# One decoder step on one core: a weight split shared by two engines, another order of the last projections and their builds, and cache pages queued ahead of a store

## What is computed

```python
h = rms_norm(x, ln_g) @ w_in          # 1024 -> 4168 columns, split into 11 parts
# A) sparse attention: an indexer scores every key, each query keeps 256
score = einsum(relu(iq . ik), iw);  idx = top_k(where(causal, score, -inf), 256)
logits = rms_norm(q) . rms_norm(k)[idx] / 8 + rel_bias[bucket(q_pos - idx)]
a_out = softmax(logits) @ v[idx]      # 8 query heads, 4 key heads of 64
# B) HGRN2 recurrence, 8 heads with a 64x64 state, chunks of positions
f = lb + (1 - lb) * sigmoid(h_f);  S = f * S + (1 - f) (x) h_i;  o = silu(h_q) . S
mix = concat(a_out * silu(a_gate), rms_norm(o) * silu(h_gate))
y = x + mix @ w_out                   # 1024 x 1024
# outputs: y, k, v, ik of prompt and sample, the final state, and the samples' states
```

## Time and profile before

| what | value |
|---|---|
| median of 3 runs | 805.73 us (801.14 to 806.96) |
| the profiled execution | 804.48 us, span 802.8 us |
| mean granted clock of PE | 0.989 of full speed |
| busy share | PE 95%, DVE 68%, ACT 52%, POOL 49% |
| PE idle by the busy time | 802.8 - 760.7 = 42.1 us |
| projections with the recurrence | to about 519 us |
| attention, samples and first output tiles | 519 to about 730 us |
| last output tiles | to the end |

### The profile page before, as it was taken

How to read it: one execution, slowest core, us unless ns; L and a number is a source line. 1 busy time by engine, 2 the same in 40 slices (tenths; PEclk the granted TensorE clock), 3 DMA queues, 4 the chain that set the end, 5 groups by cost and what they waited for, 6 DMA issues and landing times.

```text
span 802.8 us, 20221 instructions
## 1 busy us (share of the span) xinstructions
PE 760.7 (95%) x7576; PEld 704.1 (88%) x7576; DVE 542.8 (68%) x1110; ACT 420.7 (52%) x1274; POOL 396.2 (49%) x576
## 2 busy tenths in 40 slices
PE   3999999999999999999989999979799998999998
PEld 3889989899999999999988999868588878898998
DVE  3644767998999999879994846678446367555121
ACT  6765775346365686577554746554435554422110
POOL 3454735437735693579396435249932427510220
PEclk9999999999999999999999999999999999999999
DMA  8303021221102312231202345594644634341632
GB/s 282 93 21 86 14 90 41 66 66 42 53 3 80 94 47 74 80 95 47 74 28 75 124 127 166 161 253 134 155 153 140 206 122 142 124 139 55 229 101 82
DMA packets 69927, 83.57 MB, mean 104 GB/s; under 512 B 20458, under 2 KB 55962, under 8 KB 69578
## 3 DMA queue, kind: packets, MB, share of 16 engines
q1 hardware_dynamic: 65146, 68.68, 27.3%
q0 software_dynamic: 4688, 13.64, 6.1%
HBM read 64.95 MB, written 17.34 MB: 103 GB/s over the span
## 4 chain that ended last, share of the span: by engine, by line
PE 76%; POOL 8%; DVE 5%; issue 4%; ACT 4%; DMA 2%; POOLq 0%; SPq 0%; ACTq 0%; DVEq 0%
PE psum L2298 25%; PE psum L2295 16%; PE psum L1331 11%; PE psum L2214 3%; PE psum L1264 3%; PE psum L1280 3%; POOL w_low L549 2%; PE psum L2172 2%; PE psum L2191 1%; PE psum L1242 1%; PE psum L1238 1%; PE psum L2150 1%; PE psum L1244 1%; DMA page_keys<-in_cache_kt 1%; POOL page_keys L613 1%
## 5 line engine op out<-in xcount | busy, mean ns | idle before, releaser
L2298 PE MATMUL psum<-w_high,xT_high 128*128 128x256 f32 x640 | 183.2, 286 | 0.3 <-ACT stage L1804 0.3
L2298 PE MATMUL psum<-w_low,xT_high 128*128 128x256 f32 x640 | 179.8, 281 | 0.0
L2298 PE MATMUL psum<-w_high,xT_low 128*128 128x256 f32 x640 | 179.6, 281 | 0.0
L549 POOL TENSOR_TENSOR w_low<-w_raw,w_high 128x256 fp32r<-128x256 f32 (+1 forms) x144 | 105.5, 769 | 65.0 <-ACT w_high L1686 54.7
L2298 PEld LDWEIGHTS psum<-w_high,xT_high 128*128 128x128 f32 x640 | 120.4, 188 | 2.4 <-ACT stage L1804 0.5
L2298 PEld LDWEIGHTS psum<-w_high,xT_low 128*128 128x128 f32 x640 | 120.5, 188 | 0.4
L2298 PEld LDWEIGHTS psum<-w_low,xT_high 128*128 128x128 f32 x640 | 120.6, 188 | 0.0
L2295 PE MATMUL psum<-xT_high,w_high 128*128 128x384 f32 (+3 forms) x312 | 103.8, 333 | 0.9 <-POOL w_low L549 0.9
L2295 PE MATMUL psum<-xT_high,w_low 128*128 128x384 f32 (+3 forms) x312 | 100.3, 322 | 0.0
L2295 PE MATMUL psum<-xT_low,w_high 128*128 128x384 f32 (+3 forms) x312 | 100.3, 322 | 0.0
L2037 DVE TENSOR_SCALAR_CACHE_REDUCE flag_count<-scores,candidate 128x512 f16<-128x512 f32 (+2 forms) x96 | 96.9, 1009 | 0.0
(11 more groups left out here) (334 smaller groups left out, 1857.3 us busy)
## 6 DMA issues: line engine op xcount, KB each, us to landing
w_raw<-in_w_main SPq DMA_DIRECT2D x40, 512.0 KB, 4.0
x_rows<-in_x_prompt SPq DMA_DIRECT2D x8, 512.0 KB, 6.2
page_keys<-in_cache_kt SPq DMA_DIRECT2D x32, 128.0 KB, 3.9
page_keys<-in_cache_kt POOLq DMA_DIRECT2D x32, 128.0 KB, 5.7
page_values<-in_cache_v SPq DMA_DIRECT2D x32, 128.0 KB, 3.5
page_values<-in_cache_v POOLq DMA_DIRECT2D x32, 128.0 KB, 3.9
x_res<-in_x_prompt SPq DMA_DIRECT2D x32, 128.0 KB
out<-y_rows SPq DMA_DIRECT2D x32, 128.0 KB
```

Of the source, the lines that this page charges most:

```text
L549: last = gp.tensor_tensor(WL[:, u % 2, 4 * h + k, 0:w], raw(u)[:, h, k, 0:w], f(WH[:, u % 2, 4 * h + k, 0:w]), ALU.subtract)
L2298: last = pe.matmul(ps(BANK[n], w, rows(i)), x[:, k, row0(i):row0(i) + rows(i)], ww[:, sl, k, 0:w], start=first, stop=final)
```

## The change

Three things are changed.

1. The value unit's split. POOL does only the first half of unit 14, one quarter each after the jobs 1 and 4 of unit 13. DVE does the second half with four subtractions of 128x256 ahead of the last (largest) of the six masks, after waiting for POOL's half. POOL waits for DVE's half before it splits the first half of unit 15.
2. The order of the last projections and builds. The tiles come in the order 1 to 7, then 0; both units do the first three places one after the other, then alternate; the builds stand behind q = 4, 5, 7, 8, 10, 12, 14 and 16, with the row loads and key stores moved along. The low part of the bias table is made behind the seventh build. The last build (tile 0) puts its queries in PSUM bank 5, and DVE makes their low part after the row maximum of step 0. The scores of step 0 wait for seven builds' queries and begin with the upper 512 keys; the lower 512 wait for the eighth build's keys, and the transposes of step 0 for its queries.
3. POOL's queue in the attention. Page set 11 is issued right after the states' update, ahead of the padded queries (L783, L786), and the sets 13 and 15 ahead of the states' stores (L821).

```diff
+TILES = [1, 2, 3, 4, 5, 6, 7, 0]
@@ jobs(u) @@
     if u == NU - 2:
-        order = [(u, 0), (u, 1), (u, 2)]
-        for i in range(NT):
-            order += [(u + 1, i), (u, i + 3)]
-        out = [(x, "N", i, 0) for x, i in order if i < NT]
+        order = [(x, b) for x in (u, u + 1) for b in range(3)]
+        for b in range(3, NT):
+            order += [(u, b), (u + 1, b)]
+        out = [(x, "N", TILES[b], 0) for x, b in order]
...
-BUILD_AT = {JOB0[LAST] + q: i for q, i in ((4, 0), (6, 1), (8, 2), (10, 3), (12, 4), (14, 5), (15, 6), (16, 7))}
+BUILD_Q = (4, 5, 7, 8, 10, 12, 14, 16)
+BUILD_AT = {JOB0[LAST] + q: b for b, q in enumerate(BUILD_Q)}
+LOAD_Q = {BUILD_Q[b] + 1: b + 2 for b in range(NT - 2)}
+STORE_Q = {3: 0, 4: 1, 7: 2, 8: 3, 10: 4, 11: 5, 14: 6}
@@ split_half @@
             gp.wait_ge(s["weights_high_ready"], 2 * u + h + 1)
+            if (u, h) == (HGU[-1] + 2, 0):
+                gp.wait_ge(s["weights_low_ready"], 2 * u)
...
+        def quarter_at(u, q):
+            return ({1: 0, 4: 1} if u == HGU[-1] else {1: 0, 2: 1, 3: 2, 4: 3}).get(q)
@@ sample_state @@
                 last.then_inc(s["sample_state_ready"], 1)
+                load_key_pages(gp, numbers, 11)
                 gp.wait_ge(s["sample_state_ready"], 1)
@@ gp_tail @@
             sample_state()
+            for n in (13, 15):
+                load_key_pages(gp, numbers, n)
             for hh in range(2):
                 gp.dma_start(s_sample[0].rearrange("b (j a) k v -> a k (b j) v", a=2)[hh],
...
-            for n in (11, 13, 15):
-                load_key_pages(gp, numbers, n)
@@ q_parts @@
+        def q_bank(b):
+            return 3 if b < NT - 1 else 5
@@ dve_builds @@
             for i in range(NT):
-                dve_build(dve, i)
-                if i == NT - 3:
+                dve_build_keys(dve, i)
+                if i < NT - 1:
+                    dve_build_queries(dve, i)
+                if i == NT - 2:
                     dve.wait_ge(s["bias_high_ready"], 1)
...
-                if i == 2:
+                if i == 4:
                     dve_norm_sample(dve, link)
@@ dve_tail, after the row maximum of step m @@
+                    if m == 0:
+                        dve_build_queries(dve, NT - 1)
@@ pe_build @@
-            ge(pe, s["q_built"], i)
+            if b < NT - 1:
+                ge(pe, s["q_built"], b)
+            else:
+                pe.wait_ge(s["state_part_decayed"], NT * NG)
@@ scores(m) @@
-                    pe.wait_ge(s["k_built"], NT)
-                    pe.wait_ge(s["q_built"], NT)
+                    pe.wait_ge(s["q_built"], NT - 1)
+                if m == 1:
+                    pe.wait_ge(s["k_built"], NT)
...
-                for c0 in range(0, w, 512):
+                for c0 in (512, 0) if m == 0 else range(0, w, 512):
                     n = min(512, w - c0)
+                    if m == 0:
+                        pe.wait_ge(s["k_built"], NT - (c0 > 0))
@@ transposes(m) @@
                 if m == 0:
...
+                    pe.wait_ge(s["q_built"], NT)
@@ search: masks() @@
                 for k, sc, w in tiles:
+                    if k == 5:
+                        dve.wait_ge(s["weights_low_ready"], 2 * (HGU[-1] + 1) + 1)
+                        split_half(dve, HGU[-1] + 1, 1)
                     dve_mask(dve, link, k, P, sc, w, JK, CU, MSK[:, SC0[k + 2]:SC0[k + 2] + w])
```

More of the change, by code:

```diff
@@ L632, in sp_last_unit @@
         def sp_last_unit(sp, numbers, q):
[L634 to L637, removed]
+            if q in STORE_Q:
+                store_keys(sp, STORE_Q[q])
+            if q in LOAD_Q:
+                load_rows(sp, LOAD_Q[q])
             if q == 9:
@@ L843, in gp_tail, with q_parts, act_query_tile @@
             split_w(gp, NU + 3)
-        def q_parts(i):
-            c = slice(i * P, (i + 1) * P)
-            lo, hi = ps(3, 512, HD).rearrange("p (j t) -> p j t", t=P), ps(3, 512, P, HD).rearrange("p (j t) -> p j t", t=P)
+        def q_bank(b):
+            return 3 if b < NT - 1 else 5
+        def q_parts(b):
+            c = slice(TILES[b] * P, (TILES[b] + 1) * P)
+            lo, hi = (ps(q_bank(b), 512, r + HD, r).rearrange("p (j t) -> p j t", t=P) for r in (0, HD))
             return c, lo, hi
-        def act_query_tile(act, i):
-            c, lo, hi = q_parts(i)
-            act.wait_ge(s["q_rows_transposed"], i + 1)
+        def act_query_tile(act, b):
+            c, lo, hi = q_parts(b)
+            act.wait_ge(s["q_rows_transposed"], b + 1)
             act.activation(QS[0:HD, 0:AH:2, c], lo, ACT.Copy, scale=QGC[0:HD, 0:1])
@@ L962, in dve_mask, with dve_norm @@
             dve.tensor_scalar(out, flag[0:r, 0:w], -1.0, -NEG, ALU.add, ALU.mult).then_inc(s["masks_ready"], 1)
-        def dve_norm(dve, link, chain, i):
-            sl = i % 2
-            dve.wait_ge(s[f"qk_rows_in{sl}"], 32 * (i // 2 + 1))
+        def dve_norm(dve, link, chain, b):
+            i, sl = TILES[b], b % 2
+            dve.wait_ge(s[f"qk_rows_in{sl}"], 32 * (b // 2 + 1))
             q = QR[:, sl, :].rearrange("p (h d) -> p h d", d=HD)
@@ L1200, in dve_tail, with pe_build @@
                     mix_low(NT)
-        def pe_build(pe, i):
-            pe.wait_ge(s["qk_normed"], i + 1)
-            if i == 0:
+        def pe_build(pe, b):
+            pe.wait_ge(s["qk_normed"], b + 1)
+            if b == 0:
                 pe.wait_ge(s["job_copied"], JOB0[LAST])
-            ge(pe, s["k_built"], i)
+            ge(pe, s["k_built"], b)
             for j in range(KVH):
-                last = pe.transpose(ps(2, P, o=j * P), KR[:, i % 2, j, :, :].rearrange("p a d -> p (a d)"), IDN[:, :])
+                last = pe.transpose(ps(2, P, o=j * P), KR[:, b % 2, j, :, :].rearrange("p a d -> p (a d)"), IDN[:, :])
             last.then_inc(s["k_rows_transposed"], 1)
-            ge(pe, s["q_built"], i)
+            if b < NT - 1:
+                ge(pe, s["q_built"], b)
+            else:
+                pe.wait_ge(s["state_part_decayed"], NT * NG)
             for j in range(4):
-                last = pe.transpose(ps(3, P, o=j * P), QR[:, i % 2, j * P:(j + 1) * P], IDN[:, :])
+                last = pe.transpose(ps(q_bank(b), P, o=j * P), QR[:, b % 2, j * P:(j + 1) * P], IDN[:, :])
             last.then_inc(s["q_rows_transposed"], 1)
@@ L1631, in _ @@
                         load_key_pages(gp, numbers, 1)
-                    if u in HGU[1:] and 1 <= n - JOB0[u] <= 4:
-                        split_quarter(gp, u + 1, n - JOB0[u] - 1)
+                    if u in HGU[1:] and quarter_at(u, n - JOB0[u]) is not None:
+                        split_quarter(gp, u + 1, quarter_at(u, n - JOB0[u]))
             gp_tail(gp, link, numbers)
```

31 lines of the change are left out of this document (17 added, 14 removed).

## The result

The kernel after takes 798.96 us in the median (14 runs, 793.89 to 803.17), the kernel before beside it 803.78 (14 runs). The ratio is 0.9926 with the interval 0.990 to 0.9952: 4.8 us faster where 12 to 14 were forecast, and 0.5 us beyond the end of the range.

The account below looks back on a forecast made before the run. PE, 95% busy, was taken as the bound, so only its idle time and lower-clock stretches count. 804.48 us less 4.0, 4.0 and 6.3 is 790.2, with 1.2 for the median 791.4; range 787.5 to 798.5.

Parts of the forecast that it names:

- Part 1: Unit 13's jobs: two PE waits for POOL's state update and the lower clock behind them go; 4.0 us, bounds 3.0 to 4.1.
- no wait for the state update after 411 us: Sign expected in the new profile at unit 13's jobs, with the job behind it at 3.1 us.
- Part 2: Last job to attention: waits for the last two builds' keys and queries go; 4.0 us, from 2.8 to 4.4.
- all on PE's own path, and behind step 15 everything that PE meets follows its own earlier steps: Claim in the sum that the gains 4.0, 4.0 and 6.3 us add up to 790.2 us.
- Part 3: Samples' keys at step 13: the wait for page set 11 and the lower clock go; 6.3 us, at most 6.8.
- set 13's zero slack: Step 14's keys: set 13 lands at 574.0 us, just when PE wants it; 0.5 us left for it.
- the four: Rivals: set 13 late, 0.17; DVE half late, 0.1; POOL's issues stretched, 0.05; builds slower, 0.03.
- rival (2): DVE's half of the split comes late, PE waits, clock falls, part 1 gives nothing: 795.4 us; chance 0.1.
- The rule that spoke against part 3: GpSimd can't write descriptors beside two-port VectorE operations; set 11's issues would take 12.4 us, part 3 would bring nothing.
- C: Samples' keys at step 13, where PE waits 4.36 us for set 11, then runs slower; 6.3 us forecast.
- A: Jobs of unit 13, where PE waits four times, 4.4 us in all, for POOL's state update; 4.0 us forecast.
- B: Step from last job to attention, where PE waits 4.39 us for keys and queries; 4.0 us forecast.

Follow-up runs that it names:

- e1: Kernel before with part 1 of the change alone (the split shared by POOL and DVE); 800.36 us, ratio 0.9962 to before.
- e0: The changed kernel once more, no edit, for a second profile; 799.14 us, ratio 0.9936 to before.
- e6: Changed kernel with the loads of states and spread values issued by SP behind page set 2 instead of by POOL; 794.85 us, ratio 0.9886 to before.
- e12: e6 with one gap (a wait of GpSimd for its own product of queries before the weights' split); 790.74 us, ratio 0.9834 to before.
- e4: The kernel before once more, no edit, for a second profile; 807.85 us (1 run).
- e8: The kernel before once more, no edit, for a third profile; 800.49 us (1 run).
- e2: Kernel before with part 2 of the change alone (order of tiles, builds, last queries), pages as before; 805.35 us, ratio 1.002 to before.
- e7: Changed kernel with bit_kept written as scalar_tensor_tensor with two tensors; 793.63 us, ratio 0.9894 to before.
- e5: Changed kernel with GpSimd's loads of states and spread values held until page set 2 is in; 796.07 us, ratio 0.9906 to before.
- e9: Changed kernel with the edits of e6 and e7 together; 795.63 us, ratio 0.9859 to before.
- e10: e9 without part 3 of the change (sets 11, 13, 15 behind the states' stores again); 802.70 us, ratio 0.9949 to before.
- e13: e12 with a second gap, a GpSimd wait between the two halves of the split; 790.75 us, ratio 0.9833 to before.
- e3: Kernel before with part 3 of the change alone (sets 11, 13, 15 ahead of the states' stores); 802.26 us, ratio 0.999 to before.

## Why the prediction was wrong

- **Part 1** (4.0, bounds 3.0 to 4.1): right, 3.9 in the profiles and 0.38% in e1. The two waits and the lower clock went; the 1.65 us that should stay are 1.67. The half on DVE was ready at 425.5; behind the late scan everything lies 3.3 us later than in before's first profile, so that is 1.2 us ahead of the forecast's 423.4. The wait of 0.55 came from the landing, taken as 4.1 us: issued at 425.5, the raw half was there for PE at 431.6, so 6.1. In e1 it took 6.2 (PE waits 0.83), in e0, e6 and e12 4.9, 4.6 and 5.0 with no wait. The two raw halves are now issued 1.5 us apart, where it was 13.3; whether that lengthens the landing isn't shown. The sign "no wait for the state update after 411 us" was badly put: the wait of 1.39 that stays is at 413.8, as everything is 3.3 us later behind the late scan.
- **Part 2, the local gain** (4.0, bounds 2.8 to 4.4): 4.95, above the bound. Scores start 1.8 us after the last job's end (520.61 against 518.80) instead of the forecast's 2.3, and the rest of the chain is 4.46 long instead of 4.7. The new wait of 1.87 is named for the queries, ready at 524.92, but the exponential ends at 524.6 as well: the two are level, as forecast, and the queries cost 0.3. The builds cost nothing: from unit 15's samples' job to the last job it is 86.25 us in after, 86.31 in before.
- **The step that failed** is the one that was written as "all on PE's own path, and behind step 15 everything that PE meets follows its own earlier steps". The sum let PE come 4 us sooner and set only the sets 11, 13 and 15 against that. Set 2 has a start that hangs on the last job's end, like the states (`load_key_pages` waits for the last job ahead of the sets 2 and 3), and lay 0.5 us ahead of PE in the first profile, 1.4 and 5.3 in e4 and e8. Its last pages share the DMA engines with 2 MB of POOL's. Counted from the last job's matmul, its last page lands at 17.6 to 21.5 us in before's three profiles and at 19.3 to 22.1 in the four with the new order and the old loads, so it didn't move; PE came for it at 22.0 to 22.9 and now comes at 17.2 to 18.7. So part 2's gain is given back at step 3, +4.0 in the mean of after and e0. The four profiles with the new order and the old loads have waits of 4.92 (e2), 4.83 (e0), 2.24 (e7) and 0.66 us (after). In after it is that short since the lower clock at 526 to 528 us had made PE late already. e5 and e6 show the cause: with set 2 out of the way of the states the wait is gone. In the six profiles of that kind (e5, e6, e9, e10, e12, e13) the stretch through step 3 is 13.1 to 14.6 us, in the four others 15.3 to 20.8.
- **Part 3** (6.3, bounds 0.3 to 6.8): the mechanism was right. Set 11 landed in 2.6 us (3.2 taken), the wait went, set 13's zero slack was the place to watch: in e6 and e12 it costs 1.27 and 0.96 us at step 14. The term was mis-sized, since 4.36 us and the 2.5 of the lower clock came from the one execution in which the wait was longest: three profiles give a mean of 3.5 for the stretch, the six with the old order and pages one of 2.2 against e3, and the part alone gives 0.1%. It is worth 7.1 us only when PE comes sooner (e10).
- **Rivals.** None of the four happened; of rival (2) a trace is left, the 0.55 us for the raw weights, with no fall of the clock. The rule that spoke against part 3 didn't show: four issues took 2.87 to 2.92 us with DVE busy for 59 to 98%. That is no test of it, since DVE's work beside them was nearly all copies and row maxima out of PSUM. What was stretched is other work: DVE's `bit_kept` by POOL's run, and POOL's additions beside DVE's scan.
- **The base.** The first profile of before had the scan on time, 4.07 us less than its two others, and the longest wait at step 13. For the total these cancelled, so 804.48 looked typical; for single terms they didn't.

Together: the forecast's 14.3, less 4.0 given back at step 3, less 2.8 for C, less 1.3 for the scan, less 0.1 for A, plus 0.95 for B gives 7.05; the mean spans of three and two profiles differ by 7.1, the medians by 4.8. The profiled executions are not the median ones: they average 797.5 in after, whose median is 799.0, and 804.3 in before, with 803.8. At which place the other executions of after lose the last 2 us stays open.

## What to carry to other kernels

When a change lets the bound engine arrive sooner, go through every transfer whose issue hangs on the same event as the arrival, not only those that the change touches, and write down its slack. A wait for a transfer on a loaded DMA should be read in two or three executions before it is a term of a sum: here it was 4.4, 3.8 and 0 us. Put small transfers that are wanted soon ahead of large ones; here, on one queue, that was worth 4 us (e6 against after). And a mend that removes a stall in one profile isn't shown by it when the stall comes and goes by itself: look for the same instruction at its other places in that profile, as at 296.3 us in e7.

## What the runs showed of the hardware

VectorE's small instruction on six columns was kept waiting for 7.36 us, for more than one instruction of GpSimd: until its unbroken run had a gap. The run's last 12 tensor_tensor instructions take 0.7 us each, and the second of them was under way. A gap of 0.08 us let it in (e12). The counting instructions, which write an accumulator, are not held: in before's first profile 384 to 896 columns took 0.61 to 1.14 us beside the same run (209.94 to 214.0, the run ends at 213.68) and the same from 216.4 us on, without it. The Trainium skill (SBUF — State Buffer, Who interferes with whom) excepts that form; it speaks of one instruction of the other engine as the wait, the trace shows a whole run of them. Of the 14 profiles without the gap 11 have the stall at this place, at 7.34 to 7.38 us each time, and three haven't (before's first, e7, e10). Why some escape stays open: held or not, the instruction starts 1.02 to 1.05 us behind the same start of GpSimd's. At the two later places, where it is held for 3.1 to 4.6 us, none of the 14 escapes.

It goes the other way too. GpSimd's addition of two tensors, 128x256, takes 0.73 us as a rule. In the 17 profiles every one of these additions that takes over 1 us, 1.2 to 2.75, starts while VectorE runs a scan or a scalar_tensor_tensor on the samples' flags, 8x1025, and ends 0.5 to 0.6 us behind it (in e4 558.72 against 558.20).

The last page of set 2, 128 KB on SP's queue, lands in 12.7 to 17.2 us in the ten profiles in which GpSimd's 2 MB are issued beside it, and in 4.0 to 5.6 us in the seven in which they come behind it (e5, e6, e9 to e13), issued at the same place of the program.
